# A transformer kernel of 36,909 instructions: its expert routing cut shorter, two weight pieces fetched earlier, six TensorE products added

## The reference

```python
p_group = softmax(xt @ w_group)                       # 4 groups
g_w, g_idx = top_k(p_group, 1)
e_logits = (xt @ w_expert).reshape(n_tok, 4, 8)[arange(n_tok), g_idx[:, 0]]
e_w, e_idx = top_k(softmax(e_logits), 2)              # 2 experts of the group's 8
weight = g_w * e_w / sum(e_w)
expert = (g_idx * 8 + e_idx)                          # 32 experts, 1024 (token, expert) pairs
hid = silu(ragged_dot(xs, w_gate, sizes)) * ragged_dot(xs, w_up, sizes)      # 1024 -> 512
ys = ragged_dot(hid, w_down, sizes) * weight          # 512 -> 1024
return segment_sum(ys, token)
```

## Time and profile before

| | |
|---|---|
| median of 3 runs | 2795.91 us (2794.87 to 2802.02) |
| profiled execution | 2792.38 us, its span 2790.6 us |
| PE busy | 2517.8 us, 90% of the span |
| VectorE, ScalarE, GpSimd busy | 1080.6, 776.6, 181.8 us |
| mean granted TensorE clock | 0.962 of full speed |
| moved by DMA | 576.40 MB, 207 GB/s over the span |
| weights of the experts | 384 requests of 1024 KB |
| matmuls of the experts on gate and up (L1234) | 4096 records, 480.8 us busy |

### The profile page before, as it was taken

One profiled execution on the slowest core, in us unless ns is written; L12 is line 12 of the kernel. 1 busy time (PEld: TensorE's weight loads), 2 busy tenths in 40 slices (PEclk: granted clock), 3 DMA queues, 4 the chain that ended last, 5 costly groups with the idle time before them and its releaser, 6 DMA issues. The chain is left out here.

```text
span 2790.6 us, 36909 instructions
## 1 busy us (share of the span) xinstructions
PE 2517.8 (90%) x14554; PEld 1859.7 (67%) x14554; DVE 1080.6 (39%) x1602; ACT 776.6 (28%) x1235; POOL 181.8 (7%) x304
## 2 busy tenths in 40 slices
PE   9895998877898978997888799999999999999998
PEld 7574565444476665664444487788888877888887
DVE  4654110100253551110000566655551566555642
ACT  3530101000144420100010343543431453534331
POOL 0000111111100001111111000000000010000000
PEclk9996999999998978999999899999999999999999
DMA  6128999999822068999999331323232222222331
GB/s 173 46 83 322 407 407 407 412 405 407 307 69 76 9 264 348 407 406 408 412 408 400 127 108 51 121 65 101 91 136 91 84 76 81 85 91 91 106 121 53
DMA packets 174815, 576.40 MB, mean 207 GB/s; under 512 B 20496, under 2 KB 104016, under 8 KB 125042
## 3 DMA queue, kind: packets, MB, share of 16 engines
q1 hardware_dynamic: 164146, 558.07, 52.6%
q0 software_dynamic: 10560, 16.81, 1.8%
HBM read 569.56 MB, written 23.07 MB: 212 GB/s over the span
## 5 line engine op out<-in xcount | busy, mean ns | idle before, releaser
L1234 PE MATMUL ps<-first_weights,moe_xsT 128*64 128x256 f32 x2688 | 312.4, 381 | 50.8 <-DMA first_weights<-in_moe_w_up 31.5
L249 PE MATMUL ps<-l_h_hi,l_w_hi 128*128 128x512 f32 x896 | 353.0, 394 | 0.0
L251 PE MATMUL ps<-l_h_hi,l_w_lo 128*128 128x512 f32 x896 | 348.8, 389 | 0.0
L250 PE MATMUL ps<-l_h_lo,l_w_hi 128*128 128x512 f32 x896 | 348.7, 389 | 0.0
L1299 DVE TENSOR_TENSOR moe_hid<-moe_silu,ps 128x256 f32<-128x256 f32 x64 | 27.0, 421 | 795.5 <-PE ps L1234 795.5
L1234 PEld LDWEIGHTS ps<-first_weights,moe_xsT 128*64 128x64 f32 x2688 | 223.1, 137 | 149.8 <-issue 99.6
L2748 DVE TENSOR_TENSOR l_w_lo<-l_raw,l_w_hi 128x2048 fp32r<-128x2048 f32 x76 | 174.0, 2292 | 270.5 <-ACT l_w_hi L2509 270.5
L1280 ACT ACTIVATE moe_ys<-ps 128x512 f32<-128x512 f32 x64 | 38.2, 597 | 682.5 <-PE ps L1252 682.5
L1252 PE MATMUL ps<-first_weights,moe_hidT 128*64 128x512 f32 x672 | 167.0, 641 | 38.5 <-DVE moe_hidT L1301 38.5
L1234 PE MATMUL ps<-first_ring,moe_xsT 128*64 128x256 f32 x1408 | 168.4, 388 | 33.9 <-DMA first_ring<-in_moe_w_up 18.3
L2509 ACT ACTIVATE l_w_hi<-l_raw 128x2048 fp32r<-128x2048 f32 x76 | 145.5, 1918 | 179.9 <-PE ps L251 166.9
(11 more groups left out here) (562 smaller groups left out, 4351.1 us busy)
## 6 DMA issues: line engine op xcount, KB each, us to landing
first_weights<-in_moe_w_up SPq DMA_DIRECT2D x84, 1024.0 KB
first_weights<-in_moe_w_down SPq DMA_DIRECT2D x84, 1024.0 KB
first_weights<-in_moe_w_gate SPq DMA_DIRECT2D x84, 1024.0 KB
first_ring<-in_moe_w_gate SPq DMA_DIRECT2D x44, 1024.0 KB
first_ring<-in_moe_w_up SPq DMA_DIRECT2D x44, 1024.0 KB
first_ring<-in_moe_w_down SPq DMA_DIRECT2D x44, 1024.0 KB
l_raw<-in_ffn_up SPq DMA_DIRECT2D x44, 1024.0 KB, 5.1
l_raw<-in_w_in SPq DMA_DIRECT2D x22, 1024.0 KB, 5.2
```

The lines of the kernel that those rows point to most:

```text
L249: pe.matmul(out, stationary[0], moving[0], start=first, stop=False)
L250: pe.matmul(out, stationary[0], moving[1], start=False, stop=False)
L251: return pe.matmul(out, stationary[1], moving[0], start=False, stop=last)
L1234: ins = pe.matmul(k.ps[64 * h:64 * h + 64, 2 + m, 0:256], xsT[:, j, :], weights.gate_up[s][m][:, j, 256 * h:256 * h + 256], start=j == 0, ...
```

## The change

It has five parts.

1. **Shorter routing.** The logits are read from PSUM where they are used, in place of a copy. Two operations make both expert numbers. Counts and ranks are divided by 64 in f32, by scaling and by adding and subtracting 1.5 x 2^23, in place of integer shifts; the block of a pair is a minimum of two values in place of a selection. `start` is `end` shifted by one column, in one tile.
2. **The expert list** (`list_experts`) is made in the expert block, for 19 columns in place of 50, behind VectorE's first copy of `xsT`; SP waits for it (`expert_set`) ahead of the last loads.
3. **The first gather** (`first_rows`) is issued in the routing block, straight from `take`; `xs` now lies in the routing's buffers and is cleared there.
4. **Two gate pieces ahead.** `load_ahead` requests the two gate pieces of expert 3 (the fourth) into `early` when the logits are made; block 3 reads them there. The gate pieces of expert 6 (the seventh) go into set 0 when block 0 has used its own. On PE and SP the first six blocks are written out ahead of the loop.
5. **Six products** of 128x128 by 128x512 f32 into PSUM bank 6, read by nobody, stand behind the list products (`run_on`).

```diff
+    def run_on(self, pe, n):
+        for _ in range(n):
+            pe.matmul(self.ps[:, 6, :], self.ident, self.cst[:, 0:512], start=True, stop=True)
...
     def rank_and_list(self, k, pe):
         ins.then_inc(self.listed, 1)
+        k.run_on(pe, 6)
...
     def choose(self, k, dve, link, r):
+        lg = k.ps[:, 0, :].rearrange("p (t c) -> p t c", t=NT)
+        link(dve.memset(x.start[:, 0:1], float(EXPERTS)))
-        link(dve.tensor_copy(x.lg[:, :, :], k.ps[:, 0, :].rearrange("p (t c) -> p t c", t=NT)[:, :, 0:NL]))
...
-        for c in range(TOPK):
-            link(dve.tensor_copy(x.ef[:, c, :], x.ei[:, :, c]))
-            link(dve.scalar_tensor_tensor(x.ef[:, c, :], x.gf[:, :], float(PER_GROUP), x.ef[:, c, :], ALU.mult, ALU.add))
+        link(dve.tensor_copy(x.ef[:, :, :], x.ei[:, :, 0:TOPK].rearrange("p t c -> p c t")))
+        link(dve.scalar_tensor_tensor(x.ef[:, :, :], x.gf[:, :].unsqueeze(1).to_broadcast([P, TOPK, NT]), float(PER_GROUP), x.ef[:, :, :], ALU.mult, ALU.add))
...
     def lay(self, k, dve, link, r):
-        link(dve.tensor_scalar(x.cnt_i[:, :], k.ps[:, 2, 0:32], float(SLOTS - 1), None, ALU.add))
-        link(dve.tensor_scalar(x.cnt_i[:, :], x.cnt_i[:, :], 6, None, ALU.arith_shift_right))
-        link(dve.tensor_copy(x.nb[:, :], x.cnt_i[:, :]))
-        link(dve.tensor_scalar(x.nb[:, :], x.nb[:, :], -1.0, 0.0, ALU.add, ALU.max))
...
-        link(dve.tensor_tensor(x.start[:, :], x.end[:, :], x.nb[:, :], ALU.subtract))
+        link(dve.tensor_scalar(x.nb[:, :], k.ps[:, 2, 0:32], 1.0 / SLOTS, -1.0 / SLOTS - BELOW, ALU.mult, ALU.add))
+        link(dve.tensor_scalar(x.nb[:, :], x.nb[:, :], WHOLE_PART, -WHOLE_PART, ALU.add, ALU.add))
+        link(dve.tensor_scalar(x.nb[:, :], x.nb[:, :], 0.0, None, ALU.max))
...
+        link(dve.tensor_scalar(x.blk_f[:, :], x.rank_f[:, :], 1.0 / SLOTS, -BELOW, ALU.mult, ALU.add))
+        link(dve.tensor_scalar(x.blk_f[:, :], x.blk_f[:, :], WHOLE_PART, -WHOLE_PART, ALU.add, ALU.add))
+        link(dve.scalar_tensor_tensor(x.slot_f[:, :], x.blk_f[:, :], -float(SLOTS), x.rank_f[:, :], ALU.mult, ALU.add))
+        link(dve.scalar_tensor_tensor(x.base_f[:, :], x.blk_f[:, :], -1.0, x.base_f[:, :], ALU.add, ALU.add))
+        link(dve.scalar_tensor_tensor(x.blk_f[:, :], x.blk_f[:, :], float(SLOTS), x.ef[:, :, :].rearrange("p c t -> p (c t)"), ALU.mult, ALU.add))
+        link(dve.tensor_tensor(x.blk_f[:, :], x.blk_f[:, :], x.base_f[:, :], ALU.min))
...
-        dve.wait_ge(x.done, 4)
+        dve.wait_ge(x.done, 3)
+    def first_rows(self, pool, normed, r):
+        pool.wait_ge(normed, NT)
+        pool.memset(self.xs[:, :], 0.0).then_inc(self.emptied, 1)
+        pool.wait_ge(self.emptied, 1)
+        pool.wait_ge(self.x_out, 16 * NT)
+        pool.wait_ge(self.done, 2)
+        pool.indirect_dma_start(out=self.xs[:, :], out_offset=None, in_=r.x_dram,
+                                in_offset=bass.IndirectOffsetOnAxis(ap=r.take[0:SLOTS, 0:1], axis=0),
+                                bounds_check=SEQ - 1, oob_is_err=False).then_inc(r.rows_in, 16)
...
+    def load_ahead(self, sp, layer):
+        for c in range(2):
+            sp.dma_start(self.k.early[:, c, :],
+                         self.k.a["moe_w_gate"][layer, WEIGHT_SETS, c * 512:(c + 1) * 512, :].rearrange("(p j) c -> p (j c)", j=4)).then_inc(self.ahead[c], 16)
...
-            with sp.Fori(1, TURNS) as i:
+            for s in range(WEIGHT_SETS):
+                if s == 0:
+                    weights.load(sp, layer, 0, 2 * WEIGHT_SETS, free(0, 1), range(2))
+                weights.load(sp, layer, s, WEIGHT_SETS + s, free(s, 1), range(6) if s else range(2, 6))
+            for s in range(WEIGHT_SETS):
+                weights.load(sp, layer, s, 2 * WEIGHT_SETS + s, free(s, 2), range(6) if s else range(2, 6))
+            with sp.Fori(3, TURNS) as i:
...
+            sp.wait_ge(expert_set, 1)
...
-            for_each_block(pe, n, body)
+            for s in range(WEIGHT_SETS):
+                body(s, 0, s)
+            for s in range(WEIGHT_SETS):
+                body(s, 1, WEIGHT_SETS + s, ahead=s == 0)
+            for_each_block(pe, n, body, 2)
...
             dve.tensor_copy(xsT[:, :, :], k.ps[:, 0, :].rearrange("p (j s) -> p j s", j=ND)).then_inc(xsT_kept, 1)
+            rt.list_experts(k, dve, link, r, expert_set)
```

More of the change, by code:

```diff
@@ L637, in _ @@
             weights.load(sp, layer, 2, 2, lambda c: None, range(2))
+            sp.wait_ge(rt.made, NT)
+            weights.load_ahead(sp, layer)
             sp.wait_ge(rt.x_out, 16 * NT)
@@ L1075, in window_layer @@
     st.retire(k)
+    return rt
 class Routes:
@@ L1104, in __init__ @@
         self.loaded = [[st.sem(f"loaded{s}_{c}") for c in range(6)] for s in range(WEIGHT_SETS)]
+        self.ahead = [st.sem(f"ahead{c}") for c in range(2)]
         self.used = [[st.sem(f"used{s}_{c}") for c in range(6)] for s in range(WEIGHT_SETS)]
@@ L1223, in _, with gate_piece, later, body @@
             turn_rows()
-            def body(s, times, b):
+            def gate_piece(s, times, c, ahead):
+                if ahead:
+                    pe.wait_ge(weights.ahead[c], 16)
+                    return k.early[:, c, :].rearrange("p (j c) -> p j c", c=HIDDEN)
+                wait_then_tick(pe, loaded[s][c], times * 16 + 16 if s or not later(times) else times * 16, tick_pe)
+                return weights.gate_up[s][0][:, 4 * c:4 * c + 4, :]
+            def later(times):
+                return not (isinstance(times, int) and times == 0)
+            def body(s, times, b, ahead=False):
                 wait_then_tick(pe, xsT_kept, b + 1, tick_pe)
@@ L1230, in body @@
                     for j in range(ND):
[L1231 to L1232 removed]
+                        if j % 4 == 0 and m == 0:
+                            piece = gate_piece(s, times, j // 4, ahead)
+                        elif j % 4 == 0:
+                            wait_then_tick(pe, loaded[s][2 + j // 4], times * 16 + 16, tick_pe)
+                            piece = weights.gate_up[s][1][:, j:j + 4, :]
                         for h in range(2):
[L1234 removed]
+                            ins = pe.matmul(k.ps[64 * h:64 * h + 64, 2 + m, 0:256], xsT[:, j, :], piece[:, j % 4, 256 * h:256 * h + 256],
                                             start=j == 0, stop=j == ND - 1)
@@ L2988, in program @@
     weights = ExpertWeights(k, first)
-    window_layer(k, base, 0, routes[0], weights)
-    experts(k, 0, routes[0], weights, lambda n: down_piece(k, n))
-    latent_layer(k, base, 1, routes[0], routes[1], weights)
-    experts(k, 1, routes[1], weights, lambda n: in_piece(k, 0, n))
+    rt = window_layer(k, base, 0, routes[0], weights)
+    experts(k, 0, routes[0], rt, weights, lambda n: down_piece(k, n))
+    rt = latent_layer(k, base, 1, routes[0], routes[1], weights)
+    experts(k, 1, routes[1], rt, weights, lambda n: in_piece(k, 0, n))
     first.retire(k)
```

84 lines of the change are left out of this document (38 added, 46 removed).

## The result

The kernel after takes **2781.4 us** (median of 6 runs, 2775.2 to 2784.4) where the kernel before took 2795.9 (6 runs, 2794.9 to 2802.0) on the same chip. The medians differ by 14.5 us; the ratio worked out from all runs is 0.9942, with a 95% interval of 0.9932 to 0.9952, which is 16.2 us (13.4 to 19.0). A second series of the same kernel gave 0.9942 (0.9927 to 0.9956). The forecast was 2777.6 us with a gain of 18.3; the result lies in the range for all cases (2772 to 2790), 0.4 us over that of the likeliest alone (2775 to 2781), and is faster by 0.58%. The profiled execution took 2777.4 us around a span of 2775.6; the one of before, 2792.4 around 2790.6.

The account below looks back on a forecast made before the run. The weight stream was taken to bound the expert stages, with 20.6 us idle. Gains of 10.8 and 8.45 us (together 19.3), less 1 for joins, gave 18.3 us: 2777.6 us, range 2772 to 2790.

Parts of the forecast that it names:

- the likeliest alone: Whole kernel: the summed forecast of 2777.6 us, with its own range of 2775 to 2781 and chance 0.62.
- What bounds the stage: Expert stages: the weight stream sets their end; it idles 10.8 and 9.8 us, so 20.6 us can be won.
- The pieces: Hole in the weight stream before each expert stage: 2 MB fetched ahead fill 5.1 us per layer.
- The shorter routing: VectorE's routing up to the list products: 1.85 us less (1.3 to 2.0), with 0.15 added for PSUM reads.
- The expert list: Moved into the expert block: its two long operations take some 0.7 us each, hidden, and SP's new wait costs nothing.
- GpSimd's DRAIN: Routing block's end waits for it: 5.45 us long, or 8.3 us from the last indirect instruction; block 0 at 248.0 and 1052.9.
- drain from the landing: Rival, routing block's end: the 5.45 us drain follows the 6.6 us landing; gain 7.3 us, 2788.6 us; chance 0.16.
- the clock stays at half through the six products: Rival, end of routing: products end at 250.4 and 1055.0; gain 12 us, 2783.9 us; chance 0.12.
- The six products: Behind the list products: 5.4 us at full clock, keeping it up for block 0, whose first request comes 1.8 us sooner.
- The size: Both layers' holes: 10.8 us won in layer 0, 8.45 in layer 1, less 1 for joins; gain 18.3 us.
- Rows behind the whole stream: Rival, first gather: rows queue behind the weights, so the hole only moves; gain 0 to 1, 2795 us; chance 0.06.
- Slower by series of gather and drain: Rival, routing block's end: an 18.9 us landing, then the drain; 17 us slower, 2813 us; chance 0.04.

Follow-up runs that it names:

- e3: The kernel after without the two gate pieces fetched ahead, six blocks still written out; 5.9 us (3.4 to 8.4) faster than the kernel before.
- e2: The kernel before with only the two gate pieces fetched ahead and six blocks written out; 7.0 us (4.5 to 9.5) faster than the kernel before.
- c1: The kernel after unchanged, run again in a second series beside other variants; ratio 0.9942 to the kernel before.
- e4: The kernel after with the first gather and the six products moved into the expert block, its tile cleared in the routing block; 2780.4 us, ratio 0.9936.
- e7: The kernel after with nine products in place of six; the ratio did not change, and the 1 to 1.5 us expected were not seen.
- e8: As e4, but seven products ahead of the rows and one between the row transposes and the gate products; ratio 0.9942 to the kernel before.
- e9: The kernel after with eighteen products in place of six, to delay block 0; ratio 1.0001 to the kernel before.
- e5: The kernel before with only the shorter routing and the moved expert list; no measurable gain (2.2 us faster to 2.8 slower).
- e6: The kernel before plus a gather that moves nothing in each routing block, waited for before GpSimd drains; time as before.

## Why the prediction was right, and where it missed

*What bounds the stage: right.* The GB/s, the share of 1.02 between 458 and 714 us and the tail match; the stages of twelve kernels, with holes from 0.3 to 11.5 us, follow them one for one. PE eats the lead and meets the stream in after too: it waits for pieces near the end of layer 0.

```profile
718.70 1.95 PE L1283 MATMUL ps<-first_weights,moe_xsT 128*64 128x256 f32 x16 [0.55 <-DMA first_weights<-in_moe_w_up]
721.49 1.95 PE L1283 MATMUL ps<-first_weights,moe_xsT 128*64 128x256 f32 x16 [0.84 <-DMA first_weights<-in_moe_w_up]
```

*The pieces: right.* 4.9 and 5.2 us of hole, for 5.1 each (under e3), and 10.3 us between e3 and the full change, for 10.2. Put in without the earlier gather they slow block 0's rows and give some of it back (e2). Code written out cost nothing that the traces show.

*The shorter routing: right in size* (1.85 predicted; from VectorE's first copy of the logits, 222.01 and now 219.65, to the list products 15.69 became 13.62 us, so 2.07). The operations that read PSUM cost no more than their neighbours (0.17 us for the copy of 16 columns, as from SBUF before; 0.48 for the four picks, 0.55 before), where I had added 0.15. VectorE's timeline after, the group copy and the four picks:

```profile
219.65 0.17 DVE L355 COPY win_gl<-ps 128x16 f32<-128x16 f32 x1 [3.09 <-PE ps L321]
...
221.44 0.48 DVE L363 TENSOR_TENSOR win_picked<-ps,win_ohg 128x32 f32<-128x32 f32 x4
```

*The expert list: right.* Its two long operations took 0.77 us each behind VectorE's first copy, for 0.7 predicted, and nothing waits there.

*GpSimd's DRAIN: mechanism right, size short.* I put the start of block 0 at 12.15 and 12.4 us after the list products; it was 13.94 and 12.93 (c1 13.66, 13.06). The length of 5.45 us that the row showed is not a constant: 7.99 and 7.29. The second reading that the prediction gave, 8.3 us from the last indirect instruction, was the nearer. The rival "drain from the landing" fell: it puts block 0 16.9 us after the list products, 3 to 4 us later than it was. So did "the clock stays at half through the six products".

*The six products: the step that failed.* They ran on a clock that rose at 237.5 us (5.71 us for twelve records, 5.4 predicted) and in layer 1 at 1036.3 (6.55 us), but kept nothing warm: the clock was at half (0.50, 1.2 GHz) for block 0's first gate products in both layers, the request came 6.18 and 6.17 us after the transposes where 4.7 were predicted. Windows of after at the transposes and the copy behind them:

```profile
247.00:248.00 1.00, 0.79 (x7) 0.80 (x7) 0.00 (x0) 0.00 (x0) 0.00 (x0) 0.89 1.04 434
248.00:249.00 1.00, 0.42 (x4) 0.24 (x2) 0.54 (x1) 0.00 (x0) 0.18 (x1) 0.50 1.03 426
```

The clock even outlived the 4.70 us in which PE stood: the transposes of layer 0 began on it, and it fell near 247.8, before the first gate product at 249.60. In layer 1 it was down before the transposes. With DRAIN holding the block, 7.1 and 5.2 us lay between the last of the six and the first gate product. I had asked only how long PE may stand between the products and block 0, and left out that block 0 begins with transposes and a copy, 2.4 us without a product. The 3 us that I allowed, read from one fall of the clock, are no fixed length either: behind the last product it stayed up for 2.0 to 5.4 us (after, c1, e3, e4, e7).

*The size: in part luck.* Layer 0 was to have no hole and has 0.6 us, though block 0 came 1.5 us late (1.8 after the list products) and the 1.5 us of the clock weren't won. The sum with these two as measured leaves 2 to 3 us, and e7, with block 0 no nearer to the list products (13.64 us), has 2.4. What filled the rest in after and c1 is TensorE's clock ahead of the routing, which the change doesn't touch: the last transposes in front of the logits ran at full clock there and at half in before and e7. VectorE's first copy of the logits stood 10.2 us behind the request for expert 0's gate in after, 9.5 in c1, but 11.8 in before and 12.4 in e7. PE's timelines, before and then after:

```profile
215.55 1.95 PE L495 MATMUL ps<-cst,resid 128*128 128x128 f32 x8
```

```profile
214.59 1.07 PE L515 MATMUL ps<-cst,resid 128*128 128x128 f32 x8
```

Layer 1 was to keep 1.35 us and kept 3.8 and 2.9. The later start (0.5 us after the list) and the unwon clock (1.5) are 2.0 of it in after, and the same clock ahead of the routing, this time at half for longer than in c1 (12.2 us to the first copy for 11.3), is the 0.9 between the two. Had the clock held in block 0, e8 shows 0.9 us of hole. So the sum came near by errors and luck that partly cancelled; that it said 18.3 us where 16.2 were measured is itself within the interval (13.4 to 19.0). Of its signs, GpSimd's DRAIN (5 to 7 us foretold) and clock 1.0 at block 0's products did not come true.

*Rivals.* Rows behind the whole stream: fell, the rows landed 7.3 to 7.7 us after their gather began under it (e4), in layer 1 at 1042.7 while the stream ran on past 1046. The Trainium skill ("DMA: Bandwidth & Descriptors", section "Queues, rings and completion order") has each engine take turns between queues packet by packet. The traces agree that no backlog is waited for, but sharing is not free: 7.3 us against 3.5 with an ended stream. Slower by series of gather and drain: fell, the two lie side by side.

## What to carry to other kernels

Where a stream of weights sets the end, find the gaps in it and price every edit in microseconds of gap: the stages of all variants here followed that, and in e9 delay alone opened 10.3 us of gap again. A price read at one place (5.45 us for a drain, 3.5 us for a gather) holds for the load beside it; look for what will run beside the moved step. Work that is to keep the clock up has to reach to the next products, not just to the next instruction of PE: with it there the clock held in both layers (e8), with 2.8 to 3.6 us between it held in three cases of six. And one profiled execution can have a microsecond or two of luck in it; compare the distances between the events, not only the sums.

## What the hardware showed that was not expected

- GpSimd's DRAIN at a block's end took 5.37 to 5.45 us when it began 2.8 to 2.9 us behind the last indirect DMA instruction, 7.3 to 8.0 us when it began right at it with a full stream beside it, and 0.12 to 0.14 us behind an empty one 8 to 10 us old. It ended 7.0 to 8.3 us after the indirect instruction in each of the long cases. Whether it waits for the landing or counts from the instruction is left open: the landing itself isn't in the trace of after, but in e4 the same gather landed 7.3 and 7.7 us after its start, about when the DRAINs of after ended (7.0 and 7.8); and at the end of the expert stages, where the scatter had already landed, it was long all the same.
- A gather of 64 rows landed 7.3 to 7.7 us after its instruction started with the weight stream at share 1.02 (e2, e4), 6.7 to 6.8 us where the stream ended on the way (e5), and 3.0 to 3.5 us with the stream ended or ending (layer 1 of e6 and before).
- With only 1.2 us of transposes and a wait for a copy between two series of products, 2.8 to 3.6 us in all, the full clock fell in three cases (both layers of e7, layer 1 of e4) and held in three (both layers of e9, layer 0 of e4). With one product of 1.1 us between, it held in both layers of e8. What decides between falling and holding isn't shown.
- The same code ahead of the routing ran its last eight transposes in 1.07 us in one execution and 1.95 in another, as the clock had fallen late or early, and with that VectorE's first copy of the logits, and the list products behind it, moved against the weight stream. In layer 0 the copy came 9.5 to 10.2 us after the request for expert 0's gate in the six profiles with 1.07, and 11.7 to 12.4 us after it in the six with 1.95.
